# Input projections of the second and third mixer computed as three rounded products, with the gate matrix in a place of its own

## The reference, cut to what matters

```python
u = rms_norm_2(h, mix_norm[layer])
# layer 0: second mixer of the program ("hy"): latent attention beside gated linear attention
c_q, c_kv, k_r, g_q, g_k, g_v, g_a, g_r = split_cols(u @ w_in, HY_SPLITS)      # 1024 -> 432 + 3 x 512 columns
# layer 1: third mixer ("nsa"): compressed, selected and window keys, mixed by gates
q, k_c, v_c, k_s, v_s, k_w, v_w, g = split_cols(u @ w_in, NSA_SPLITS)          # 1024 -> 5 x 512 + 48 columns
gates = sigmoid(g)
```

## Time and profile before

| | |
|---|---|
| runs shown | 3, median 2359.17 us (2353.51 to 2361.3) |
| profiled execution | 2354.99 us, of which the span of its instructions is 2353.2 us |
| granted TensorE clock, mean | 0.974 of full speed |
| TensorE busy | 2185.1 us (93%) |
| VectorE, ScalarE, POOL busy | 983.2, 621.5, 21.7 us |
| second mixer up to its attention | 1468 to 1547 us of the span |
| third mixer up to its attention | 1976 to 2073 us of the span |

### The profile page before, as it was taken

How to read it: one execution, slowest core, us unless ns; L and a number is a source line. 1 busy time by engine, 2 the same in 40 slices (tenths; PEclk the granted TensorE clock), 3 DMA queues, 4 the chain that set the end, 5 groups by cost and what they waited for, 6 DMA issues and landing times.

```text
span 2353.2 us, 26648 instructions
## 1 busy us (share of the span) xinstructions
PE 2185.1 (93%) x10858; PEld 1290.7 (55%) x10858; DVE 983.2 (42%) x1721; ACT 621.5 (26%) x1012; POOL 21.7 (1%) x38
## 2 busy tenths in 40 slices
PE   5989988998899899989876999989999999999998
PEld 3447752333333333333323888568887886557887
DVE  6971232222222222212214555365555553375555
ACT  3021110111011001001103443354435433065433
POOL 0000000000000000000000000000000000100000
PEclk8999989999999999999998999999999999999999
DMA  7771469999999999999997543324544543312541
GB/s 308 264 284 70 151 267 410 427 423 428 428 422 428 427 427 420 428 427 421 424 428 306 198 178 142 143 88 187 209 161 170 206 166 143 143 55 108 215 166 76
DMA packets 42926, 633.66 MB, mean 269 GB/s; under 512 B 5040, under 2 KB 5040, under 8 KB 6224
## 3 DMA queue, kind: packets, MB, share of 16 engines
q1 hardware_dynamic: 42800, 631.90, 65.5%
HBM read 630.84 MB, written 1.05 MB: 269 GB/s over the span
## 4 chain that ended last, share of the span: by engine, by line
PE 72%; DMA 17%; DVE 4%; ACT 2%; issue 1%; SPq 0%; ACTq 0%; DVEq 0%
DMA piece<-in_moe 17%; PE bank L1994 11%; PE bank L1889 10%; PE bank L1891 10%; PE bank L1890 10%; PE bank L2029 5%; PE bank L643 5%; PE bank L1270 2%; PE bank L1975 2%; PE bank L2053 2%; PE bank L937 1%; PE bank L1307 1%; PE bank L1274 1%; PE bank L2330 1%; PE bank L1084 1%
## 5 line engine op out<-in xcount | busy, mean ns | idle before, releaser
L1994 PE MATMUL bank<-piece,xeT 128*64 128x512 f32 (+1 forms) x2304 | 451.4, 626 | 61.9 <-DMA piece<-in_moe 55.4
L1895 DVE TENSOR_TENSOR ffn_lo<-slot,ffn_hi 128x2048 fp32r<-128x2048 f32 x132 | 302.1, 2292 | 149.3 <-ACT ffn_hi L2455 143.9
L1994 PEld LDWEIGHTS bank<-piece,xeT 128*64 128x64 f32 (+1 forms) x2304 | 135.8, 132 | 344.9 <-issue 323.3
L1889 PE MATMUL bank<-ffn_hi,hT_hi 128*128 128x512 f32 x704 | 279.5, 397 | 9.1 <-DVE hT_lo L567 6.7
L2455 ACT ACTIVATE ffn_hi<-slot 128x2048 fp32r<-128x2048 f32 x132 | 251.7, 1913 | 122.6 <-PE bank L1891 122.6
L1891 PE MATMUL bank<-ffn_hi,hT_lo 128*128 128x512 f32 x704 | 275.1, 391 | 0.0
L1890 PE MATMUL bank<-ffn_lo,hT_hi 128*128 128x512 f32 x704 | 274.4, 390 | 0.0
L2102 DVE TENSOR_TENSOR hT<-hT,bank 128x512 f32<-128x512 f32 x144 | 92.2, 682 | 264.0 <-PE bank L2053 263.9
L2150 DVE TENSOR_SCALAR work<-bank 128x256 f32<-128x256 f32 x60 | 25.5, 425 | 350.5 <-PE bank L2001 350.5
L1889 PEld LDWEIGHTS bank<-ffn_hi,hT_hi 128*128 128x128 f32 x704 | 132.6, 188 | 38.5 <-issue 12.3
L1891 PEld LDWEIGHTS bank<-ffn_hi,hT_lo 128*128 128x128 f32 x704 | 132.4, 188 | 28.5
(11 more groups left out here) (645 smaller groups left out, 2435.6 us busy)
## 6 DMA issues: line engine op xcount, KB each, us to landing
piece<-in_moe SPq DMA_DIRECT2D x192, 2048.0 KB, 24.5
slot<-in_ffn SPq DMA_DIRECT2D x44, 3072.0 KB, 10.3
slot<-in_ada SPq DMA_DIRECT2D x16, 1024.0 KB, 5.4
slot<-in_merge SPq DMA_DIRECT2D x4, 3072.0 KB, 12.2
slot<-in_nsa_in SPq DMA_DIRECT2D x5, 2048.0 KB, 7.4
slot<-in_ada SPq DMA_DIRECT2D x2, 3072.0 KB, 18.0
slot<-in_w_in SPq DMA_DIRECT2D x6, 1024.0 KB, 7.1
slot<-in_hy_in SPq DMA_DIRECT2D x3, 2048.0 KB, 8.1
```

Source lines behind the costliest of these rows:

```text
L1889: pe.matmul(out, left[0], right[0], start=start, stop=False)
L1895: return dve.tensor_tensor(lo, x, hi.bitcast(F32), ALU.subtract)
L1994: pe.matmul(bank[n * c:n * (c + 1), :], x[:, kt, :], w[i][:, at:at + 512], start=kt == 0, stop=False)
```

## The change

- In both mixers `project_tensor` gives way to `in_products_tensor`, which does half a unit (four kt) in three rounded products. A block's weights are parted in halves: ScalarE writes the high part of a half (`in_weights_high`) in a free `end`, or in the second mixer also in `cat_hi`; VectorE writes the low part over the plain weights in the slot (`in_weights_low`). The eight halves of the second mixer and the ten of the third are placed one by one between the existing work of the two engines.
- The activations are made in high and low parts by `ffn_norm_scalar` and `ffn_norm_vector`. VectorE therefore does both halves after ScalarE, and the first product waits for both parts of the first half. The last addition to `x` before the mixer comes after the first half's low parts.
- The order of the third mixer's units changes: both token tiles of a half follow each other, (j, half, t), and some small products sit between other units than before.
- The gate matrix and two small matrices are loaded early, on their own, into the `rope` table's place (`nsa_s`). The gates need plain float32 activations: POOL adds the high and low parts (`sum_rows`), and `gates_tensor` comes right after block 0 and waits for that sum.
- The slot of `nsa_c` is free after `cmp_h` instead of `cmp_kv`.
- The low parts of the third mixer's output weights move from before the attention into it, one of four in each second batch (`beside`).

```diff
-            item("nsa_c", ("nsa_c", 0), 4096 + 384 + 128, (sig["cmp_kv"], 2))
+            item("nsa_c", ("nsa_c", 0), 4096, (sig["cmp_h"], 1))
...
+def in_weights_high(k, act, e, j, half):
+    s = k["sig"]
+    it = k["plan"][e.names[j]]
+    act.wait_ge(k["landed"][it.slot], it.landed)
+    for sem, at in e.ready(k, j, half):
+        act.wait_ge(sem, at)
+    act.activation(in_high(k, e, j, half), in_plain(k, e, j, half), ACT.Copy).then_inc(s["in_w_hi"], 1)
+def in_weights_low(k, dve, e, j, half):
+    s = k["sig"]
+    dve.wait_ge(s["in_w_hi"], e.at + 2 * j + half + 1)
+    low_part(dve, in_low(k, e, j, half), in_plain(k, e, j, half), in_high(k, e, j, half)).then_inc(s["in_w_lo"], 1)
+def in_products_tensor(k, pe, e, j, t, half):
+    s = k["sig"]
+    n, u = e.ncols[j], e.base + 2 * j + t
+    pe.wait_ge(s["in_w_hi"], e.at + 2 * j + half + 1)
+    pe.wait_ge(s["in_w_lo"], e.at + 2 * j + half + 1)
+    if half == 0 and j >= 2:
+        pe.wait_ge(s["proj_act"] if t == 0 else s["proj_dve"], (u - 4) // 2 + 1)
+    if j == 0 and t == 0:
+        pe.wait_ge(s["hT_act"], 2 * e.norm + half + 1)
+        pe.wait_ge(s["hT_dve"], 2 * e.norm + half + 1)
+    for kk in range(4):
+        if j == 0 and t == 0 and half == 0 and kk == 2:
+            stream_turn_tensor(k, pe, e.norm, 1)
+        kt = 4 * half + kk
+        h = [k[part][:, kt, t * P:(t + 1) * P] for part in ("hT_hi", "hT_lo")]
+        w = [part(k, e, j, half)[:, kk * n:(kk + 1) * n] for part in (in_high, in_low)]
+        mm = split_product(pe, k["ps"][u % 4][:, 0:n], h, w, kt == 0, kt == KT - 1)
+    if half == 1:
+        mm.then_inc(s["proj_ready"], 1)
...
+def hy_rooms_free(k, j, half):
+    s = k["sig"]
+    if j >= 2:
+        return [(s["proj_ready"], HY_BASE + 2 * (j - 2) + 2)]
+    if half == 1:
+        return [(s["down_done"], downs_at(0, FFN_LAST))] if j else [(s["ffn_down_lo"], FFN_STEPS)]
+    return []
...
+def nsa_rooms(k, j, half):
+    return k["ends"][(2 * j + half) % 3]
...
+def sum_rows(k, pool):
+    s = k["sig"]
+    pool.wait_ge(s["hT_act"], 2 * 6 + 2)
+    pool.wait_ge(s["hT_dve"], 2 * 6 + 2)
+    for half in range(2):
+        kts = slice(4 * half, 4 * half + 4)
+        k["pos"].mark(pool.tensor_tensor(k["hT_sum"][:, kts, :], k["hT_hi"][:, kts, :].bitcast(F32), k["hT_lo"][:, kts, :].bitcast(F32), ALU.add))
+    k["pos"].wait()
+    pool.drain().then_inc(s["rows_pool"], 1)
```

The third mixer's program of VectorE, first part:

```diff
+            in_weights_low(third, dve, NSA_IN, 0, 0)
-            for u in range(4):
+            for u in range(3):
                 ffn_add_vector(k, dve, 2, u)
-            mixer_norm_vector(k, dve, 6, gain["mix", 1])
+            ffn_norm_vector(third, dve, 6, gain["mix", 1], 0)
+            ffn_add_vector(k, dve, 2, 3)
+            ffn_norm_vector(third, dve, 6, gain["mix", 1], 1)
+            in_weights_low(third, dve, NSA_IN, 0, 1)
+            in_weights_low(third, dve, NSA_IN, 1, 0)
+            token_scale_vector(k, dve, 6)
             nsa_read(third, dve, 1, 0)
+            in_weights_low(third, dve, NSA_IN, 1, 1)
             cmp_clear_vector(third, dve)
             nsa_turn_read(third, dve, 1, 5)
             cmp_blocks_vector(third, dve)
+            in_weights_low(third, dve, NSA_IN, 2, 0)
             nsa_read(third, dve, 1, 1)
+            in_weights_low(third, dve, NSA_IN, 2, 1)
             cmp_hidden_vector(third, dve)
+            in_weights_low(third, dve, NSA_IN, 3, 0)
             nsa_read(third, dve, 1, 2)
+            in_weights_low(third, dve, NSA_IN, 3, 1)
```

The third mixer's program of TensorE, first part:

```diff
-            nsa_project_tensor(third, pe, 1, 0)
+            nsa_project_tensor(third, pe, (0, 0, 0), (0, 0, 1), (0, 1, 0), (0, 1, 1))
+            gates_tensor(third, pe)
+            nsa_project_tensor(third, pe, (1, 0, 0), (1, 0, 1))
...
-            gates_tensor(third, pe)
-            nsa_project_tensor(third, pe, 1, 1)
-            nsa_project_tensor(third, pe, 2, 0)
+            nsa_project_tensor(third, pe, (1, 1, 0), (1, 1, 1), (2, 0, 0), (2, 0, 1))
             cmp_blocks_tensor(third, pe)
-            nsa_project_tensor(third, pe, 2, 1)
+            nsa_project_tensor(third, pe, (2, 1, 0), (2, 1, 1))
             cmp_heads_tensor(third, pe)
-            nsa_project_tensor(third, pe, 3, 0)
-            pe.wait_ge(s["rows_pool"], 2)
+            nsa_project_tensor(third, pe, (3, 0, 0), (3, 0, 1), (3, 1, 0))
+            pe.wait_ge(s["rows_pool"], 3)
             pe.wait_ge(s["rows_dve"], 4)
             turn_one(third, pe, turns[2], 5)
```

More of the change, by code:

```diff
@@ L1168, in attend_vector @@
             maxima(batches[n + 2])
+        if beside is not None and n in beside:
+            beside[n]()
         if n >= 2 and batches[n - 2].last and u.low is not None:
@@ L2566, with hy_rooms, hy_project_tensor @@
 HY_HALF = HY_T // 2
-def hy_project_tensor(k, pe, j, t, lo=0, hi=KT):
-    at = (2 * j + t) * KT
-    project_tensor(k, pe, [f"hy{i}" for i in range(4)], HY_BASE, [HYA, 512, 512, 512], k["hT"], KT, HY_BASE, part=range(at + lo, at + hi))
+def hy_rooms(k, j, half):
+    if half == 0:
+        return k["ends"][k["plan"][f"hy{j % 2}"].slot]
+    return k["cat_hi"][:, :, :].rearrange("p a b -> p (a b)") if j % 2 else k["ends"][k["plan"]["lora"].slot]
+def hy_rooms_free(k, j, half):
[5 more added lines that the diff above has]
+    return []
+HY_IN = Entry([f"hy{j}" for j in range(4)], [HYA, 512, 512, 512], HY_BASE, 3, 0, hy_rooms, hy_rooms_free)
+def hy_project_tensor(k, pe, j, t, halves=(0, 1)):
+    for half in halves:
+        in_products_tensor(k, pe, HY_IN, j, t, half)
 def hy_read(k, eng, t, j):
@@ L2991, in gates_tensor, with cmp_blocks_tensor @@
     s = k["sig"]
+    pe.wait_ge(s["small_loaded"], 64)
+    pe.wait_ge(s["rows_pool"], 2)
+    for t in range(TT):
+        for kt in range(KT):
+            mm = pe.matmul(k["ps"][6][:, t * 48:(t + 1) * 48], k["hT_sum"][:, kt, t * P:(t + 1) * P], k["nsa_s"][:, kt * 48:(kt + 1) * 48], start=kt == 0, stop=kt == KT - 1)
+    mm.then_inc(s["gate_in"], 1)
+def cmp_blocks_tensor(k, pe):
+    s = k["sig"]
     it = k["plan"]["nsa_c"]
@@ L3480, in _ @@
             ffn_weights_high(k, act, 0, 0, 0)
-            ffn_scalar(k, act, 0, gain["ffn", 0])
-            mixer_norm_scalar(k, act, 3, gain["mix", 0])
+            ffn_scalar(k, act, 0, gain["ffn", 0], lambda: in_weights_high(second, act, HY_IN, 0, 0))
+            for half in range(2):
+                ffn_norm_scalar(second, act, 3, gain["mix", 0], half)
+            in_weights_high(second, act, HY_IN, 0, 1)
+            in_weights_high(second, act, HY_IN, 1, 0)
+            stream_squares_scalar(k, act, 3)
+            in_weights_high(second, act, HY_IN, 1, 1)
             hy_read(second, act, 0, 0)
@@ L3651, in _ @@
             nsa_turn_read(third, dve, 9, 1)
[L3652 removed]
+            attend_vector(third, dve, nsa, HD ** -0.5, beside={3 + 2 * i: (lambda pair: lambda: out_weights_low(third, dve, NSA_OUT, 0, (pair,)))(pair) for i, pair in enumerate(NSA_OUT.pairs)})
             out_weights_low(third, dve, NSA_OUT, 1)
@@ L3695, in _ @@
             ffn_tensor(k, pe, 0, nxt=3)
-            project_tensor(second, pe, [f"hy{j}" for j in range(4)], HY_BASE, [HYA, 512, 512, 512], k["hT"], KT, HY_BASE, part=range(2 * KT), norm=3)
-            hy_project_tensor(second, pe, 1, 0, 0, 4)
+            for half in range(2):
+                for t in range(TT):
+                    hy_project_tensor(second, pe, 0, t, (half,))
+            hy_project_tensor(second, pe, 1, 0, (0,))
             pe.wait_ge(s["proj_act"], HY_BASE // 2 + 1)
@@ L3729, in _ @@
             turns = nsa_turn_jobs(third)[0]
-            project_tensor(third, pe, [f"nsa{j}" for j in NSA_ORDER], NSA_BASE, [512] * 5, k["hT"], KT, NSA_BASE, part=range(2 * KT), norm=6)
-            nsa_project_tensor(third, pe, 1, 0)
+            nsa_project_tensor(third, pe, (0, 0, 0), (0, 0, 1), (0, 1, 0), (0, 1, 1))
+            gates_tensor(third, pe)
+            nsa_project_tensor(third, pe, (1, 0, 0), (1, 0, 1))
             pe.wait_ge(s["proj_act"], NSA_BASE // 2 + 1)
@@ L3786, in _ @@
             mla_rows(second, pool, k["pos"], 0, s["rows_pool"], second["tmp_pool"])
+            sum_rows(third, pool)
             pool.wait_ge(s["proj_act"], NSA_BASE // 2 + 3)
```

129 lines of the change are left out of this document (90 added, 39 removed).

## The result

The changed kernel takes 2368.55 us (median of 8 runs, 2359.74 to 2369.32), the kernel before 2357.88 us in runs beside it (8 runs, 2353.51 to 2361.39): ratio 1.0038, 95% interval 1.0025 to 1.0051. That is 10.7 us slower, outside the range given. In later runs the kernel before had medians of 2358.9 to 2359.1 us. The profiled execution took 2364.62 us, 3.9 us under its kernel's median, with a span of 2362.8 us.

The account below looks back on a forecast made before the run. The prediction took TensorE to bound the kernel. Second mixer 3.1 plus third mixer 2.7 minus 0.8 for the clock gave 5.0 us less, 2354.2 us on the median; range 2350 to 2358 us.

Parts of the forecast that it names:

- Second mixer: Second mixer: of 11.3 us saved on TensorE, 8.2 go to waits, so its attention starts 3.1 us sooner.
- the one on the slow side: Second mixer: VectorE's queue becomes the bound, TensorE 11.7 us late at the keys, 2369 us in all; chance 0.12.
- Third mixer's waits: Third mixer, TensorE: query rows 3.5 us, compressed heads 2.3, softmax 2.4; gates 1 if VectorE gets the port first.
- The port hardly matters: Third mixer: POOL's additions run in gaps and rotations overlap; it wins 7.5 us, 2348.6 us in all; chance 0.22.
- the walk: Both mixers: the four engines' queues followed instruction by instruction with profiled durations, VectorE and POOL taking turns.
- the 2.7 us won: Third mixer up to its attention: last unit ends 2.2 to 3.3 us sooner than 2068.1, taken as 2.7.
- I count half of one, 0.8 us: Third mixer, query transposes: a second clock dip like the 1.6 us one after the compressed scores, counted half.
- The rival on the clock: Low stretch behind each wait of 2 us or more: query rows, softmax, half 1; 4 us more, 2358 us; chance 0.16.
- The argument against it: Second mixer: a wait of 1.95 us left the clock at 1.00, held against low stretches following waits.
- The cover: Third mixer's attention: low parts of 1.16 us each cost nothing where VectorE has 1.8 us before the next maxima.
- without that cover 4 x 1.16 = 4.6 us: Third mixer's attention: cost of the output weights' four low parts if VectorE's idle time did not hide them.
- a longer attention of the third mixer: Sign of a wrong prediction: the third mixer's attention was to last as long as today.

Follow-up runs that it names:

- e1: Kernel before with only the second mixer's part of the change: 2356.96 us, ratio 0.9987.
- e9: Changed kernel with the output weights' low parts still in the attention, but ahead of the maxima on VectorE's queue: 2358.59 us, ratio 1.0001.
- e5: Changed kernel with the compression products behind both tiles of block 2's second half, ScalarE's and VectorE's queues ordered to suit: 2358.86 us, ratio 0.9999.
- e12: Changed kernel with the compression products later and the output weights' low parts ahead of the maxima: 2353.79 us, ratio 0.9980.
- e7: Changed kernel with two pairs of output weights parted ahead of the compressed softmax, two behind it, none in the attention: 2357.70 us, ratio 0.9992.
- e2: Kernel before with only the third mixer's part of the change, output weights' low parts in its attention included: 2370.68 us, ratio 1.0044.
- e11: Changed kernel with compression products later, low parts ahead of the maxima, and tile 1 of block 4's first half behind the compressed scores: 2347.20 us, ratio 0.9954.
- e6: Kernel before with one edit: the output weights' four low parts moved into the third mixer's attention: 2365.68 us, ratio 1.0028.
- e4: Changed kernel with ten unused products before each of TensorE's two long waits in the third mixer: 2366.46 us, ratio 1.0029.

## Why the prediction was wrong

**Second mixer, right.** Forecast 3.1 us sooner, measured 2.5 in the trace, and 2 to 3 by e1. The read of tile 1 of `hya` came at 1483.96 to 1484.6 (forecast 1484 to 1485). The last wait grew from 1.95 to 2.60 us; the waits for half 1 and the low weights were 1.3 and 1.0. VectorE's queue did not become the bound there: that rival, the one on the slow side, is out.

**Third mixer's waits, right in place and near in size.** Query rows 2.9 for 3.5, compressed heads' turn 1.0 for 2.3, softmax 3.1 for 2.4, gates 0.95 for 1.0. The rotations and POOL ran in turns as walked: VectorE's steps of 512 columns took 1.78 us, POOL's two additions 8.95 us together in turns with the subtractions (forecast 2.4 each), and the query transposes began at 2038.34, which is 2040.8 by the kernel before's time (forecast 2040.2). "The port hardly matters" is out by the same rows. One term came out by luck: with the walk's own durations its last unit ends at 2065.9 only if every half unit takes 2.72 us, so the 2.7 us won leave out the dip of 1.66 us that stands in the 2068.1 beside it. The changed kernel's profile happens to lack that dip; e9's has it. By the Trainium skill (SBUF — State Buffer, Who interferes with whom) the loser is blocked for the whole instruction; the 2.35 us of a two-column operation beside POOL's addition agrees. That instruction has one SBUF input, and by the page such a one contends only in a two-port mode; no run here tells which mode it was in.

**The clock, the first failed step.** "I count half of one, 0.8 us". Three low stretches followed the new waits: 2.8 us behind the query rows, 2.5 behind the softmax, 3.06 in the attention. The price was taken from the earlier trace rows, where 16 instructions took 1.66 us more; there only part of the stretch was at half clock. A whole one of 7 us costs 2.5 to 3. The rival on the clock had the place of two of them and the wrong price; behind its third, half 1, TensorE waited 1.2 us and the clock stayed at 1.00. As a rule it fails too, by the waits of 3.05 us in e5 and e12. The argument against it, a 1.95 us wait that left the clock at 1.00, proved little. That window ended at 1547 us, 0.8 us behind the wait; in the kernel before two more waits follow, and the next windows are low (TensorE's rows, then the windows):

```profile
1547.34 0.64 PE L1032 MATMUL bank<-consts,mk_h 128*96 128x128 f32 x4 [0.50 <-ACT mqT_h L1043]
1549.51 2.80 PE L1032 MATMUL bank<-consts,mk_h 128*96 128x128 f32 x12 [1.52 <-DVE mqT_h L1047]
```

```profile
1545.00:1550.00 5.00, 1.78 (x11) 1.26 (x12) 4.27 (x8) 2.19 (x4) 0.00 (x0) 0.93 0.94 403
1550.00:1555.00 5.00, 4.13 (x24) 3.45 (x23) 1.42 (x3) 1.88 (x2) 0.00 (x0) 0.73 0.34 147
```

The clock fell at 1549 us (0.57 from 1549 to 1553), behind three waits of 1.95, 0.50 and 1.52 us, and nothing tells which of them brought it. The Trainium skill (TensorE: Matmul & The Clock Gate, What's actually happening) has matmuls at 1.2 and 2.4 GHz; the spacings of 0.43 and 0.23 us, a factor of 1.9, are near that.

**The cover, the step that turned the sign.** "The output weights' low parts in the attention are 1.16 us each, put where VectorE has 1.8 us before the next maxima". Two errors are in it. The 1.81 us were read in a low stretch: at the full clock TensorE comes back sooner and the gap is 1.09 us. And the diff puts them behind the maxima, ahead of the normalisation, not before the maxima. The price that stood beside it, "without that cover 4 x 1.16 = 4.6 us", was right (3.9 us, for the last was partly hidden), but it was no rival and had no chance, and the low stretch it brings was not in it. Alone, in the kernel before, it cost 6.7 us, where the forecast had nothing; taken out of the changed kernel (e7) or put ahead of the maxima (e9), it leaves a kernel level with the one before. The prediction had named a longer attention of the third mixer as a sign of being wrong, and that is what came.

**The sum again.** -2.5 second mixer; third mixer -2.7 as walked, +5.3 for two low stretches, +1.2 as the rest that is not settled (measured +3.8); attention +3.9 inserts, +3.1 and +1.4 low clock. That gives 9.7 us, against 9.6 us in the spans and 10.7 in the medians. It adds up one execution: the terms for the third mixer ahead of its attention would be 2.6 us smaller by e2's profile and 4.6 by e9's, with the same code there.

**What stays open.** By the ratios the three orders gain 8.7 us (e9), 9.2 (e5) and 6.1 (e12 to e11), 24 in all, where together they give 19.8 (e11). The waits that they take away are 4.5, 3.8 and 3.1 us, so they come to 1.9, 2.4 and 2.0 times their waits, with intervals that reach from less than the wait to three times it. Theory A's reason for the double, a low stretch behind each wait, holds in the attention (e6, e9), but not behind the softmax wait of e5 and e12, and fillers gave back little (e4). Why the medians show so much more than the waits stays open there, and the profiles, one execution each, can't tell.

## What to carry to other kernels

Price a wait of TensorE by its length, and allow as much again for the clock: in the changed kernel's profile waits of 3 us and a train of 1.2 us waits, one in each pair of units, cost 1.7 to 1.8 times their length, but another wait of 3 us left the clock up. Profile the same code more than once before a few us are explained: the same stretch took 93.7, 95.7 and 98.3 us here. Read the idle gap that is to hide new work at the full clock, and check on which side of the instruction that TensorE waits for the new work stands: swapping two statements was worth about 9 us by the medians (some 4 to 14), 6.5 of them seen in the attention. When products get shorter, reorder what covered the other engines' chains: with the diff's arithmetic untouched, three changes of order turned 0.4% slower into 0.5% faster.

## What the runs showed of the hardware that was not expected

- A low clock stretch came with waits of 1.19 us, 8.1 us apart (behind one of them in e4, four in e2), as well as with one wait of 2.9 us, and didn't come for 8 us behind one of 3.05 us (e5, e12). How long it lasts varies: at the same wait of 2.6 us ahead of the second mixer's attention the clock was at 0.50 for 7 us in the changed kernel (1543.5 to 1550.3 us) and for 20 us (1545 to 1565 us) in e1. This is part of why single profiles and medians differ by some us.
- A vector instruction on 2 columns took 2.35 us beside a POOL addition of 1024 columns, and 0.16 us without it.
- With filler matmuls of 2.4 us the clock was 1.00 behind the softmax wait, and the kernel gained some 2 us: less than the intervals can tell. That the fillers kept it up isn't shown, for in e5 and e12 it stayed up without them.
